# Two transformer blocks on one core: the modulation tiles' silu row in SBUF, U in all eight PSUM banks, a mix ring of eight banks

## The reference

```python
def ada_params(cond, w_mod, b_mod):
    m = jax.nn.silu(cond) @ w_mod + b_mod            # six vectors of 1024
    return jnp.split(m[:, None, :], N_MOD, axis=-1)

def modulate(h, g, shift, scale):
    return rms_norm(h, g) * (1 + scale) + shift

def fourier_mix(a, w_out):
    ag = a.reshape(B, L, FNET_GROUPS, FNET_GROUP_DIM)            # 4 groups of 256
    f = jnp.fft.fft2(ag, axes=(1, 3), norm="ortho").real
    return f.reshape(B, L, D) @ w_out

a_lat = modulate(h_lat, g_norm_mix, sh1, sc1)
h_lat = h_lat + gt1 * fourier_mix(a_lat, w_fnet_out)
h_lat = h_lat + gt2 * conv_ffn(modulate(h_lat, g_norm_ffn, sh2, sc2), ...)
```

## Time and profile before

| | |
|---|---|
| median of 3 runs | 1587.09 us (1587.07 to 1587.58) |
| the profiled execution | 1586.35 us |
| its span, first to last instruction | 1584.6 us |
| mean granted clock of TensorE | 0.99 |

### The profile page before, as it was taken

One profiled execution on the slowest core, in us unless ns is written; L12 is line 12 of the kernel. 1 busy time (PEld: TensorE's weight loads), 2 busy tenths in 40 slices (PEclk: granted clock), 3 DMA queues, 4 the chain that ended last, 5 costly groups with the idle time before them and its releaser, 6 DMA issues.

```text
span 1584.6 us, 19400 instructions
## 1 busy us (share of the span) xinstructions
PE 1546.0 (98%) x7016; PEld 1283.3 (81%) x7016; DVE 780.4 (49%) x880; ACT 308.7 (19%) x481; POOL 1002.5 (63%) x790
## 2 busy tenths in 40 slices
PE   7879999999999999999999999999999999999996
PEld 6778888887887888888888888888888888888885
DVE  6695555557306665424244664565477444343014
ACT  6422111110102001112021232221222111111011
POOL 3733666667666666766647466576467766676664
PEclk9989999999999999999999999999999999999998
DMA  9991333333233333333323222232233333332321
GB/s 359 343 296 44 104 93 93 99 100 92 94 106 93 93 93 105 94 104 93 89 82 94 78 81 84 86 93 79 70 92 101 96 93 96 102 93 94 105 94 53
DMA packets 228726, 172.44 MB, mean 109 GB/s; under 512 B 5200, under 2 KB 204112, under 8 KB 228688
## 3 DMA queue, kind: packets, MB, share of 16 engines
q1 hardware_dynamic: 228688, 171.91, 35.4%
HBM read 169.80 MB, written 2.10 MB: 108 GB/s over the span
## 4 chain that ended last, share of the span: by engine, by line
PE 89%; DVE 2%; POOL 1%; ACT 0%; issue 0%; DVEq 0%; ACTq 0%; POOLq 0%
PE ps L545 30%; PE ps L549 30%; PE ps L548 30%; POOL w_lo L523 0%; DVE act_lo L1281 0%; DVE tmp L1287 0%; DVE gates L1628 0%; DVE act_lo L1386 0%; POOL w_hi L521 0%; DVE tmp L1382 0%; PE ps L832 0%; DVE res L1614 0%; DVE res L1409 0%; PE ps L651 0%; DVE tmp L1609 0%
## 5 line engine op out<-in xcount | busy, mean ns | idle before, releaser
L523 POOL TENSOR_TENSOR w_lo<-raw,w_hi 128x1024 fp32r<-128x1024 f32 x248 | 622.7, 2511 | 20.7
L545 PE MATMUL ps<-act_hi,w_hi 128*128 128x512 f32 (+1 forms) x1296 | 506.0, 390 | 5.1 <-DVE act_lo L1386 4.6
L548 PE MATMUL ps<-act_hi,w_lo 128*128 128x512 f32 (+1 forms) x1296 | 501.4, 387 | 0.0
L549 PE MATMUL ps<-act_lo,w_hi 128*128 128x512 f32 (+1 forms) x1296 | 501.4, 387 | 0.0
L520 POOL TENSOR_TENSOR w_hi<-raw,zero 128x1 fp32r<-128x1 f32 x248 | 56.9, 229 | 503.5 <-PE ps L545 503.5
L545 PEld LDWEIGHTS ps<-act_hi,w_hi 128*128 128x128 f32 x1296 | 243.7, 188 | 59.0 <-issue 5.4
L548 PEld LDWEIGHTS ps<-act_hi,w_lo 128*128 128x128 f32 x1296 | 244.0, 188 | 50.4 <-issue 1.4
L549 PEld LDWEIGHTS ps<-act_lo,w_hi 128*128 128x128 f32 x1296 | 243.9, 188 | 49.3
L521 POOL TENSOR_SCALAR w_hi<-raw 128x1023 fp32r<-128x1023 f32 x248 | 269.2, 1085 | 0.0
L545 PE MATMUL ps<-wide_hi,w_hi 128*128 128x512 f32 (+2 forms) x624 | 240.3, 385 | 2.2 <-POOL w_lo L523 1.7
L548 PE MATMUL ps<-wide_hi,w_lo 128*128 128x512 f32 (+2 forms) x624 | 239.4, 384 | 0.0
(11 more groups left out here) (193 smaller groups left out, 1452.4 us busy)
## 6 DMA issues: line engine op xcount, KB each, us to landing
raw<-in_w_in SPq DMA_DIRECT2D x88, 512.0 KB, 4.0
raw<-in_w_ffn_up SPq DMA_DIRECT2D x44, 512.0 KB, 3.9
gates<-in_w_mod_t SPq DMA_DIRECT2D x20, 1024.0 KB, 8.4
raw<-in_w_ffn_down SPq DMA_DIRECT2D x22, 512.0 KB, 3.8
raw<-in_w_ff_gate SPq DMA_DIRECT2D x22, 512.0 KB, 3.9
raw<-in_w_ff_up SPq DMA_DIRECT2D x22, 512.0 KB, 3.9
raw<-in_w_ff_down SPq DMA_DIRECT2D x22, 512.0 KB, 3.7
raw<-in_w_r_out SPq DMA_DIRECT2D x16, 512.0 KB, 3.5
```

Of the source, the lines that this page charges most:

```text
L523: nc.gpsimd.tensor_tensor(w_lo[:, two, :], raw[:, slot, :], f32(w_hi[:, two, :]), SUB).then_inc(split_done, 1)
L545: ins = mm(o, w, a, start=start, stop=False)
L548: mm(o, wl, a, start=False, stop=False)
L549: return mm(o, w, al, start=False, stop=stop)
```

## The change

Three things. The 32 tiles of chunks 1, 2, 4 and 3, and VectorE's four of chunk 0, read the row from SBUF. U takes all eight banks, tiles 6 and 7 in the banks of the spread row, and the two copies go; TensorE waits before tile 6 for ScalarE's copy of the row. The banks of F are in another order, the odd features wait for two `u_made` fewer each, the later ones have a wait of their own, and the mix uses eight banks: its first eight tiles wait for no residual, tiles 8 to 11 for residuals 2, 3, 6 and 7.

```diff
-U_BANKS = 6
-F_BANK = (4, 6, 2)
+F_BANK = (2, 4, 6)
-FNET_RING = 6
-FNET_BANKS = [2 + n % FNET_RING for n in range(len(FNET_TILES))]
+FNET_BANKS = (0, 1, 6, 7, 2, 3, 4, 5, 6, 7, 4, 5)
+FNET_FREE = (0,) * 8 + (3, 4, 7, 8)
@@ u_tile
-            return tmp[:, 5 + m, :] if m < 2 else u_bank(m)
-        def u_bank(m):
-            return ps[:, 2 + m % U_BANKS, :]
+            return ps[:, (2 + m) % 8, :]
@@ TensorE
-            for m in (6, 7):
-                pe.wait_ge(u_copied, m - 5)
-                dft_tokens([m])
+            pe.wait_ge(silu_row_copied, 1)
+            dft_tokens([6])
+            dft_tokens([7])
             for m in range(3):
-                pe.wait_ge(u_made, 2 * m + 4)
+                pe.wait_ge(u_made, 2 * m + 2)
                 features(f_odd(m), m, 1, half, half)
             for m in range(3, KT):
                 pe.wait_ge(f_made, 3 * (m - 2))
+                pe.wait_ge(u_made, m // 2 * 2 + 2)
             for n, (m, t_) in enumerate(FNET_TILES):
-                if n == 0:
-                    pe.wait_ge(f_made, 3 * (KT - 2))
-                if n >= FNET_RING:
-                    pe.wait_ge(fnet_free, n - FNET_RING + 1)
+                if FNET_FREE[n]:
+                    pe.wait_ge(fnet_free, FNET_FREE[n])
@@ ScalarE
-            for m in range(2):
-                act.wait_ge(u_done, m + 1)
-                do(u_tile(m), u_bank(m), ACT.Identity).then_inc(u_copied, 1)
@@ VectorE, mod_tile
-                nc.vector.tensor_tensor_reduce(out=w, in0=w, in1=rope_flat if c == 5 else silu_psum, scale=scale,
+                nc.vector.tensor_tensor_reduce(out=w, in0=w, in1=rope_flat, scale=scale,
```

More of the change, by code:

```diff
@@ L243, in build @@
         res_scaled, keys_done, key_scale_made = sem("res_scaled"), sem("keys_done"), sem("key_scale_made")
-        u_done, u_copied, udc_hi_made, udc_made, u_hi_made, u_made = (
-            sem(n) for n in ("u_done", "u_copied", "udc_hi_made", "udc_made", "u_hi_made", "u_made"))
+        u_done, udc_hi_made, udc_made, u_hi_made, u_made = (
+            sem(n) for n in ("u_done", "udc_hi_made", "udc_made", "u_hi_made", "u_made"))
         f_done, f_q_copied, f_made, f_hi_made, f_ready = (
@@ L576, in dft_tokens @@
                     for m in tiles:
-                        ins = product(u_bank(m), xr_hi[:, k, m * P:(m + 1) * P], xr_lo[:, k, m * P:(m + 1) * P],
+                        ins = product(u_tile(m), xr_hi[:, k, m * P:(m + 1) * P], xr_lo[:, k, m * P:(m + 1) * P],
                                       wide_hi[:, S_DFT + k, :], wide_lo[:, S_DFT + k, :], k == 0, k == TT - 1)
@@ L939, in u_hi @@
             def u_hi(m):
-                if m < 2:
-                    act.wait_ge(u_copied, m + 1)
                 act.wait_ge(u_done, m + 1)
```

## The result

The changed kernel takes 1609.44 us (median of 4 runs, 1608.11 to 1609.89) against 1587.12: slower by 22.3 us, ratio 1.014 with an interval of 1.0124 to 1.0156. The forecast was 1608.7 us, the range 1599 to 1617. The execution that was profiled took 1609.75 us, span 1608.0, that is 23.4 more than the one of before in either measure.

The account below looks back on a forecast made before the run. In the opening a chain through VectorE, not TensorE, was taken as the bound. Terms 9.0 + 5.2 + 7.4 = 21.6 us on the profiled 1586.35 gave 1607.95; with 0.74 for the runs' median, 1608.7 us, range 1599 to 1617.

Parts of the forecast that it names:

- first stretch: VectorE from 19.97 to 44.8 us: modulation tiles held by GpSimd make L1255 end later, +9.0 us (7 to 11).
- second stretch: 57.45 to 80.74 us: held chunk-2 tiles delay the last mix panel and the first add, +5.2 us (+3 to +10).
- third stretch: 80.74 to 108.5 us: GpSimd's four splits hold VectorE's tiles and adds, +7.4 us (+4 to +9.5).
- The price of a held tile: Modulation tile behind GpSimd's full 1024-wide subtraction ends 2.12 us later than unheld, 3.39 against 1.27 us.
- The rival of unfair turns: GpSimd's back-to-back products and splits keep VectorE out for two instructions: +14 us, 1623 us; chance 0.06.
- the one without any hold: Early tiles differ from chunk 5's and are not held: 1587 us, at best 1585; chance 0.05.
- the absorbing one: Later stretches absorb most, VectorE's 9.42 us of idle time swallowing held tiles: 1602 us, down to 1598; chance 0.09.
- TensorE's wait for L1255: Sign in the opening: the wait for the last piece of U ends near 53.8 and is longer than 10 us.
- The one before mix tile 10: Sign in the mix: a gap of TensorE of more than 10 us before mix tile 10.
- the ring: Mix tiles in eight banks with later residual waits for tiles 10 and 11: 0, bounds 0 to 3 us.
- the landing of the last mix panel: Time from SP's issue to use, ahead of ScalarE's squares: 5 us estimated, half of the old 9.6 us.
- U in eight banks: Opening: two ScalarE copies (1.28 us) go, `u_lo` of tiles 0 and 1 read PSUM and can't be held: 0.

Follow-up runs that it names:

- The changed kernel with fills: Changed kernel with GpSimd's SBUF-reading instructions, from the table split to the first four up splits, replaced by zero fills of the same tiles: 1581.94 us.
- the row alone: Kernel before with one edit, all modulation tiles read the row from SBUF; U, F and the mix keep banks, copies and waits: 1611.38 us, ratio 1.0152.

## Why the prediction was right

The mechanism was the one forecast, and the sizes came near. By its own steps, with what each measured in the profiled executions (all differences to before):

| step | forecast | measured | from |
|---|---|---|---|
| first tile starts | 0 | +0.4 | 20.37, 19.97 |
| first stretch, to the end of L1255 | +9.0 | +8.7 | 53.87, 44.74 |
| features, to the first chunk-2 tile | 0 | +0.7 | 67.23, 57.45 |
| second stretch, to the first add | +5.2 | +6.4 | 96.93, 80.74 |
| third stretch, to the first reciprocal | +7.4 | +6.7 | 131.44, 108.53 |
| norm, to the second reciprocal | 0 | +0.5 | 147.13, 123.76 |
| sum | 21.6 | 23.4 | spans 1608.0, 1584.6 |

That the medians lie 0.7 us from the forecast is in part luck: the steps of the profiled pair sum to 1.8 more than forecast, with misses both ways. And the 0.4 us of the first line are not the change's: in the eleven traces here the first tile starts anywhere from 18.90 to 20.61 us, with no edit ahead of it.

The price of a held tile, read from eight late ones, carried it: 3.39 us was forecast, and the twelve longest tiles of the opening took 3.25 to 3.51, most of them 3.35 to 3.42. The turns are fair, one instruction each, also where GpSimd has four products or four splits in a row. The rival of unfair turns is out by that, the one without any hold by the whole trace, the absorbing one by 23.4 us.

One of the signs named beforehand came out smaller: TensorE's wait for L1255 was to be longer than 10 us and was 9.7, as 5.2 us of its waiting fell before the odd features, on U. The one before mix tile 10, more than 10 us, came as said (15.4), though the sum of the terms had the ring at 0: it ends no chain.

What was mis-sized. **The second stretch**: I put 5 us for the landing of the last mix panel; it took 6.3 to its rounding, which is the 1.2 us. Tile 5 itself was where I had it: 84.88, that is 75.1 without the 9.8 us by which the stretch began late, against 75.0. **The clock of TensorE**, which I left out of the sum. The rows below give busy time and count by engine, and as third number from the end the granted clock as a share of 2.4 GHz, first for the 6 us from the start of the even features, then for 12 us of the norm; before and after:

```profile
44.80:50.80 6.00, 6.00 (x35) 6.00 (x36) 2.46 (x9) 2.52 (x7) 2.04 (x2) 0.67 1.06 379
112.00:124.00 12.00, 11.70 (x73) 10.70 (x74) 6.98 (x18) 4.37 (x9) 0.00 (x0) 0.86 0.71 179
```

```profile
53.90:59.90 6.00, 5.97 (x29) 5.97 (x30) 2.47 (x9) 2.19 (x5) 2.00 (x2) 0.54 0.81 261
135.00:147.00 12.00, 12.00 (x70) 11.50 (x71) 6.65 (x17) 4.33 (x9) 0.00 (x0) 0.73 0.71 179
```

At 1.2 GHz in place of 2.4 for more of those 6 us (0.54 in place of 0.67 on the mean), the features hand over 0.7 us later. The other traces say what this goes with. The four kernels that read chunks 1 and 0 from SBUF beside GpSimd's reads wait 8.3 to 9.7 us for the last piece of U; their clock in the 6 us behind it is 0.50 to 0.54, and from the end of that piece to the first chunk-2 tile it is 13.4 to 13.7 us. The seven others wait 4.8 to 6.7 us, have 0.58 to 0.74 and take 12.3 to 13.1. No run changed the length of the wait alone.

The last 0.5 us, in the norm, goes with 0.73 in place of 0.86, but not with the length of the wait before tile 10. The changed kernel with fills waits only 1.7 us there and has the same 0.73 and 15.7 us from the first reciprocal to the second; the row alone waits 4.6 us and then 9.8 and has 0.86 and 15.2, as before. What sets the clock in this place is open.

**U in eight banks at 0** was right against the kernel before, where these two `u_lo` took 0.75 us, but only half the story: with the row in SBUF it saves 2.9 us of the first stretch, since otherwise they would be held. The prediction had noted that they can't be held and priced the edits one by one, each against the kernel before. **The third stretch** has 0.7 us less than the sum of single holds: of 10.3 us forecast 9.6 came, 3.4 on adds (the longest 2.81 in place of 0.69, at 107.61) and 6.2 on tiles.

## What to carry to other kernels

Before an operand of a busy VectorE instruction is moved from PSUM to SBUF, count its SBUF inputs and look at what GpSimd does at that time: here the second SBUF input cost an instruction of 1.27 us up to 2.2 more, and it also slowed GpSimd. Eight later occurrences of the same instruction in the trace of before were enough to price it. The other way round, a hold like L1255's is found by a duration that doesn't fit the size (2.08 us for 8 columns), and is undone by the order of GpSimd's work.

## What the runs showed of the hardware

Fills by GpSimd (0.96 us for 1024 columns) held no two-input instruction of VectorE: in the kernel with fills 32 tiles stayed within 1.276 to 1.345 us. VectorE's instructions with one input in PSUM and one in SBUF (L1208 after, 0.73 us; the tiles of before) are not held by GpSimd's products. The Trainium skill says both ("SBUF — State Buffer", section Who interferes with whom: a VectorE instruction with two SBUF inputs contends with a GpSimd instruction that reads SBUF, not with one that only writes it, and one with at most one SBUF input, outside the two-port modes, does not contend), and these runs agree. Unexpected was how even the turns are: with both engines queued without a break, about 3.4 us for each tile behind a subtraction, never the time of two of GpSimd's.
